# Two transformer blocks: memory projections done inside latent attention, and RWKV head sums as two rounded products of a split operand

## The reference, cut to what matters

```python
# first_block, each of the two layers: four kinds of attention, 4 heads of 64 channels each
out_mla = _causal_softmax_attention(q_full, k_full, v_mla, mla_scale)      # latent attention
mkv = einsum('bmd,dc->bmc', mem_n, w_mem_kv[l])                            # 256 memory rows -> keys, values
mem_logits = einsum('bhsd,bhmd->bhsm', heads(mq), mk) * head_scale         # mq: 256 columns of h_res @ w_in
out_mem = einsum('bhsm,bhmd->bhsd', softmax(mem_logits), mv)

# second_block, rwkv7_mixer: sums over the 64 channels of a head
kk = kk / max(sqrt(sum(kk * kk, -1)), 1e-12)                               # "norm"
y = wkv7_scan(r, decay, k, v, -kk, kk * a)
mu = mean(y, -1); var = mean((y - mu) ** 2, -1)                            # "mean", "var"
y = (y - mu) * rsqrt(var + GN_EPS) * gn_w + gn_b
y = (y + sum(r * k * r_k, -1) * v) * g                                     # "bonus"
```

## Time and profile before

| | |
|---|---|
| median of 3 runs | 3862.49 us (3860.55 to 3867.43) |
| the profiled execution | 3867.74 us, its span 3866.0 us |
| mean granted TensorE clock | 0.987 of 2.4 GHz |
| busy share of the span | PE 94%, DVE 41%, ACT 30%, POOL 26% |
| the pairs stage | about 2003 to 2760 us of the span |
| first-block layers, mla to mem | 454 to 578 us, and the same again from 1219 us |

### The profile page before, as it was taken

How to read it: one execution, slowest core, us unless ns; L and a number is a source line. 1 busy time by engine, 2 the same in 40 slices (tenths; PEclk the granted TensorE clock), 3 DMA queues, 4 the chain that set the end, 5 groups by cost and what they waited for, 6 DMA issues and landing times. The chain is left out here.

```text
span 3866.0 us, 69669 instructions
## 1 busy us (share of the span) xinstructions
PE 3647.5 (94%) x29888; PEld 2831.3 (73%) x29888; DVE 1590.0 (41%) x3026; ACT 1169.6 (30%) x2230; POOL 1008.1 (26%) x1676
## 2 busy tenths in 40 slices
PE   6899999998999999999889999999999999999998
PEld 5664667986656679779767777776787688888886
DVE  6634545445355444521764444444003452212123
ACT  2436333014363331201644444443111221101011
POOL 4120005231200051332022222221332133434342
PEclk9999999999999999999999999999899999999999
DMA  4131201211211012212110000000222211111122
GB/s 157 45 99 40 67 18 60 89 67 65 77 53 54 23 55 99 111 44 77 50 38 19 26 25 26 29 27 19 80 66 89 94 44 55 44 47 52 44 67 97
DMA packets 190204, 225.93 MB, mean 58 GB/s; under 512 B 20990, under 2 KB 168000, under 8 KB 187080
## 3 DMA queue, kind: packets, MB, share of 16 engines
q1 hardware_dynamic: 189896, 221.47, 17.5%
HBM read 188.89 MB, written 32.56 MB: 57 GB/s over the span
## 5 line engine op out<-in xcount | busy, mean ns | idle before, releaser
L200 POOL CAST weights_high<-weights_value 128x256 fp32r<-128x256 f32 x272 | 112.7, 463 | 1121.0 <-DMA weights_value<-in_w_in_dram 930.3
L218 PE MATMUL banks<-h_high,weights_high 128*128 128x512 f32 x608 | 238.5, 392 | 8.0 <-PEq L852 5.9
L218 PE MATMUL banks<-h_high,weights_low 128*128 128x512 f32 x608 | 236.7, 389 | 0.0
L4101 POOL CAST ffn_weights_high<-ffn_weights_value 128x256 fp32r<-128x256 f32 x256 | 103.8, 454 | 466.6 <-DMA ffn_weights_value<-in_w_ff_dram 356.3
L204 POOL TENSOR_TENSOR weights_low<-weights_value,weights_high 128x256 fp32r<-128x256 f32 x272 | 212.6, 818 | 2.8
L218 PE MATMUL banks<-ffn_in_high,ffn_weights_high 128*128 128x512 f32 x512 | 199.8, 390 | 5.1 <-PEq L4348 3.1
L4474 ACT ACTIVATE hidden_value<-banks 128x512 f32<-128x512 f32 x64 | 38.3, 598 | 537.9 <-PE banks L218 537.8
L218 PE MATMUL banks<-ffn_in_high,ffn_weights_low 128*128 128x512 f32 x512 | 199.2, 389 | 0.0
L218 PE MATMUL banks<-ffn_in_low,ffn_weights_high 128*128 128x512 f32 x512 | 199.2, 389 | 0.0
L218 PE MATMUL banks<-ffn_weights_high,hidden_high 128*128 128x512 f32 x512 | 199.2, 389 | 0.0
L218 PE MATMUL banks<-ffn_weights_low,hidden_high 128*128 128x512 f32 x512 | 199.2, 389 | 0.0
(11 more groups left out here) (498 smaller groups left out, 9274.3 us busy)
## 6 DMA issues: line engine op xcount, KB each, us to landing
ffn_weights_value<-in_w_ff_dram SPq DMA_DIRECT2D x32, 1024.0 KB, 5.4
weights_value<-in_w_in_dram SPq DMA_DIRECT2D x24, 1024.0 KB, 5.3
attention_scratch<-in_ada_w_dram SPq DMA_DIRECT2D x12, 1024.0 KB, 5.3
pair_weights_value<-in_w_in_dram SPq DMA_DIRECT2D x24, 512.0 KB, 4.1
ndow_weights_value<-in_w_in_dram SPq DMA_DIRECT2D x10, 1024.0 KB, 5.1
weights_value<-in_w_out_dram SPq DMA_DIRECT2D x8, 1024.0 KB, 5.3
gates_value<-in_w_in_dram SPq DMA_DIRECT2D x16, 512.0 KB, 5.2
first_mixed<-in_ada_w_dram SPq DMA_DIRECT2D x6, 1024.0 KB, 7.0
```

What stands on the lines that cost most here:

```text
L200: last = nc.gpsimd.tensor_copy(high[:, i, :], value[:, i, :])
L218: mm = nc.tensor.matmul(out, x, y, start=(first and i == 0 and j == 0), stop=(last and i == n - 1 and j == 2))
L4101: last = nc.gpsimd.tensor_copy(high[:, i], value[:, i])
```

## The change

**First block.** The stage `mem_project` is gone. Its six groups are a list `ahead`, given to the mla `pair_attention`: PE runs them right after `do_scores(0)`, in banks 4 to 7, and ACT moves all six after the exponents of unit 0. The 12 matmuls of `hold_clock` in that stage are gone. C_MQ is loaded and split one stage earlier, in `latent_heads`; C_MK and C_MV are loaded in the mla stage, C_GATE after the six groups. The memory queries and keys lie in other buffers.

**Pairs.** A head sum is four f32r matmuls 128x512: the rounded ones times the high and the low part of the operand. Each sum needs one ACT copy (rounding) and one DVE subtraction, 128x1024 each, ahead of it. PE's mean stands after `fill(3)` instead of before `fill(2)`, the variance after a `fill(2)` instead of before it. DVE's `logs` stand behind level 1, and ACT's square of y behind a later move.

```diff
+            if ahead:
+                sp.wait_ge(ahead_done, len(ahead))
+                w.load(sp, then_load)
...
+            def do_ahead(i):
+                chunk, pairs, n, move = ahead[i]
+                if i >= 4:
+                    pe.wait_ge(ahead_moved, i - 3)
+                    pe.wait_ge(w.loaded[chunk], 16)
+                gemm(nc, k.bank(4 + i % 4, n), pairs).then_inc(ahead_done, 1)
...
                     hold_clock(k, k.psum[:, 4, 0:P], quiet[0])
+                    for i in range(len(ahead)):
+                        do_ahead(i)
+                if it == 1 and ahead:
+                    pe.wait_ge(ahead_moved, len(ahead))
...
+                    for i, (chunk, pairs, n, move_ahead) in enumerate(ahead):
+                        act.wait_ge(ahead_done, i + 1)
+                        move_ahead(k.bank(4 + i % 4, n)).then_inc(ahead_moved, 1)
...
-SLOT_OF = {C_FL: 4, C_FQ: 0, C_FK: 1, C_FV: 3, C_OUT + 2: 2, C_OUT + 3: 3}
+SLOT_OF = {C_FL: 4, C_FQ: 0, C_FK: 1, C_FV: 3, C_MQ: 0, C_MK: 1, C_MV: 5, C_OUT + 2: 2, C_OUT + 3: 3}
...
-    mem_turned_bufs = [turned_bufs[0], flat(qt[:, 2:4, :])]
+    mem_turned_bufs = [turned_bufs[0], flat(qt[:, 0:2, :])]
...
+    def mem_query(tile, half):
+        rows = mem_queries[tile][:, half * HALF:(half + 1) * HALF]
+        return C_MQ, over_tokens(b, C_MQ, tile * P, P, half), HALF, moving(nc, "act", rows, -HEAD_SCALE)
+
+    def mem_key(tile):
+        pairs = [(W.value(C_MK)[:, i, tile * P:(tile + 1) * P], b.memt[:, i, :]) for i in range(KT)]
+        return C_MK, pairs, MEM, moving(nc, "act", b.mem_keys[:, tile, :])
+
+    ahead = [mem_query(tile, half) for tile in range(2) for half in range(2)] + [mem_key(tile) for tile in range(2)]
     pair_attention(k, "mla" + tag, (weight_bufs, turned_bufs), half_of(qt), half_keys(kt), own, pair_tile(2), CAUSAL_UNITS,
-                   diagonal=k.causal_add, prefetch=(C_MQ, C_MK), splits=(C_MQ,), w=W, turned_part=turned_part, quiet=(12, 0))
-
-
-    groups = paired(qt, C_MQ, 0, -HEAD_SCALE)
-    for tile in range(2):
-        groups.append((C_MK, (0, P, MEM), [(W.value(C_MK)[:, i, tile * P:(tile + 1) * P], b.memt[:, i, :]) for i in range(KT)],
-                       "dve", moving(nc, "dve", kt[:, tile, 0:MEM])))
+                   diagonal=k.causal_add, prefetch=(C_MK, C_MV), w=W, turned_part=turned_part, ahead=ahead, then_load=C_GATE)
+
+    def mem_half(p, e, t):
+        return mem_queries[p][64 * e:64 * e + 64, t * P:(t + 1) * P]
+
     mem_values = [([(b.memt[:, i, t * P:(t + 1) * P], W.value(C_MV)[:, i, :]) for i in range(KT)], values[:, t, :]) for t in range(2)]
-    project_stage(k, "mem_project" + tag, groups, W, loads=(C_MV,), prefetch=(C_GATE,))
-    pair_attention(k, "mem" + tag, (weight_bufs, mem_turned_bufs), half_of(qt), half_keys(kt), own, pair_tile(3), MEM_UNITS,
+    pair_attention(k, "mem" + tag, (weight_bufs, mem_turned_bufs), mem_half, half_keys(b.mem_keys), own, pair_tile(3), MEM_UNITS,
...
+            b.W.load(sp, C_MQ)
...
+            b.W.split(pool, (C_MQ,), weights_rounded, weights_split)
+            pool.wait_ge(weights_split, 1)
...
+    front_high, front_low = k.over("front_sums_high", [P, S], turned_at), k.over("front_sums_low", [P, S], level_at)
+    out_high, out_low = k.over("out_sums_high", [P, S], k.x_at + 4 * S), k.over("out_sums_low", [P, S], k.x_at + 8 * S)
...
-            def by_head_ones(key, p, src):
+            def by_head_ones(key, p, high, low):
                 b = back_bank(key, p)
                 for half in range(2):
-                    mm = nc.tensor.matmul(k.bank(b + half), k.head_ones, src[:, half * HALF:(half + 1) * HALF], start=True, stop=True)
+                    s = slice(half * HALF, (half + 1) * HALF)
+                    nc.tensor.matmul(k.bank(b + half), ones[:], high[:, s], start=True, stop=False)
+                    mm = nc.tensor.matmul(k.bank(b + half), ones[:], low[:, s], start=False, stop=True)
                 mm.then_inc(back_done, 1)
...
-                wait_freed(pe, "y", p)
-                by_head_ones("mean", p, ya)
+                pe.wait_ge(out_split, 2 * p + 1)
+                by_head_ones("mean", p, out_high, out_low)
             def variance(p):
-                pe.wait_ge(y_square, p + 1)
-                by_head_ones("var", p, yb)
+                pe.wait_ge(out_split, 2 * p + 2)
+                by_head_ones("var", p, out_high, out_low)
...
-                by_head_ones("norm", p, sq)
+                pe.wait_ge(front_split, 2 * p + 1)
+                by_head_ones("norm", p, front_high, front_low)
             def bonus_sum(p):
-                pe.wait_ge(bonus_in, p + 1)
-                by_head_ones("bonus", p, bonus[p % 3])
+                pe.wait_ge(front_split, 2 * p + 2)
+                by_head_ones("bonus", p, front_high, front_low)
...
+                fill(3)
                 if p:
                     mean(p - 1)
-                fill(2)
...
+                    fill(2)
                     if lev == 2 and p:
                         variance(p - 1)
-                    fill(2)
...
+            def norm_split(p):
+                dve.wait_ge(front_rounded, 2 * p + 2)
+                nc.vector.tensor_tensor(front_low[:], sq, front_high[:], ALU.subtract).then_inc(front_split, 1)
+
+            def bonus_split(p):
+                dve.wait_ge(front_rounded, 2 * p + 3)
+                nc.vector.tensor_tensor(front_low[:], bonus[p % 3], front_high[:], ALU.subtract).then_inc(front_split, 1)
+
+            def mean_split(p):
+                dve.wait_ge(out_rounded, 2 * p + 1)
+                if p + 1 < PAIRS:
+                    wait_freed(dve, "v_tok", p + 1)
+                nc.vector.tensor_tensor(out_low[:], ya, out_high[:], ALU.subtract).then_inc(out_split, 1)
+
+            def var_split(p):
+                dve.wait_ge(out_rounded, 2 * p + 2)
+                nc.vector.tensor_tensor(out_low[:], yb, out_high[:], ALU.subtract).then_inc(out_split, 1)
...
+                    mean_split(o)
                     centre(o)
+                if is_back:
+                    level(p, 1)
                 if is_front:
                     logs(f)
+                if is_out:
+                    var_split(o)
                 if is_back:
-                    level(p, 1)
                     level(p, 2)
...
+                    norm_split(f)
...
                     directions(f)
+                    bonus_split(f)
...
+                nc.scalar.mul(kk, kx, col(5, p))
+                nc.scalar.copy(front_high[:], sq).then_inc(front_rounded, 1)
...
+            def bonus_rounded(p):
+                act.wait_ge(bonus_in, p + 1)
+                nc.scalar.copy(front_high[:], bonus[p % 3]).then_inc(front_rounded, 1)
+
+            def mean_rounded(p):
+                wait_freed(act, "y", p)
+                nc.scalar.copy(out_high[:], ya).then_inc(out_rounded, 1)
+
+            def squared(p):
+                wait_freed(act, "mean", p)
+                step(nc.scalar.activation(yb, ya, ACT.Square))
+
+            def var_rounded(p):
+                nc.scalar.copy(out_high[:], yb).then_inc(out_rounded, 1)
...
+                        mean_rounded(o)
                     if p == 0:
                         act.wait_ge(oat_away, 16)
                     move("k_tok", p, k_tok)
                     move("v_tok", p, v_tok)
-                if is_out:
-                    wait_freed(act, "mean", o)
-                    nc.scalar.activation(yb, ya, ACT.Square).then_inc(y_square, 1)
-                if is_back:
...
+                                squared(o)
...
+                            var_rounded(o)
...
+                            bonus_rounded(f)
```

More of the change, by code:

```diff
@@ L807, in pair_attention @@
 def pair_attention(k, name, bufs, q, key, value, out, pair_units, diagonal=None, bias=None, bias_here=(),
-                   prefetch=(), w=None, splits=(), turned_part=None, late=(), late_weights=None, quiet=(0, 0)):
+                   prefetch=(), w=None, splits=(), turned_part=None, late=(), late_weights=None, quiet=(0, 0),
+                   ahead=(), then_load=None):
     nc = k.nc
@@ L1146, in first_block @@
         over_slot(3, scratch_at + 2 * S * 4, scratch_at + 4 * S * 4)
+        forget_at = k.next_place()
         w_high.append(k.sb("weights_forget_high", [P, KT, FORGET_COLS], F32R, ctx=own))
         w_two.append(k.twofold("weights_forget", [P, KT, FORGET_COLS], own))
+        over_slot(5, low_t_at, low_t_at)
+        mem_keys = k.over("mem_keys", [P, 2, MEM], forget_at, F32)
         gate_sigmoids = k.over("gate_sigmoids", [P, KT, S], heads_at, F32)
@@ L1978, in _ @@
             sp.sem_clear(arrived)
+            b.W.load(sp, C_MQ)
+        @block.gpsimd
+        def _(pool):
+            b.W.split(pool, (C_MQ,), weights_rounded, weights_split)
+            pool.wait_ge(weights_split, 1)
         @block.tensor
@@ L3017, in rwkv @@
     inv = k.sb("inverse", [P, S], ctx=scope)
+    turned_at = k.next_place()
```

(16 more changed lines are left out.)

23 lines of the change are left out of this document (13 added, 10 removed).

## The result

The changed kernel took 3837.16 us (median of 4 runs, 3829.41 to 3842.26) against 3861.52 before (3857.77 to 3867.43): the ratio is 0.9937, interval 0.9917 to 0.9957, so 24.4 us less with an interval of 17 to 32. The prediction was 3834 in a range of 3820 to 3850, and faster. Its profiled execution took 3837.41 us (span 3835.6); set against the profiled execution of before, 3867.74, that is 30.3.

What follows compares the result with a forecast made beforehand. PE, busy 94% of the span, was taken as the bound. 10.5 + 18.6 + 1.8 - 1.0 = 29.9, rounded to 28.5 for small waits, gave 3834 us from 3862.5, range 3820 to 3850.

Steps and rivals of the forecast that it cites:

- First block, 10.5: Two layers' mla and mem stages: clock matmuls, a 1.47 us wait and one stage edge go, 5.27 us each, 10.5 together.
- A sum gives 0.90: Head sums in the pairs: four f32r matmuls take PE 0.91 us instead of 1.81, so 0.90 less each.
- Inner pairs, 18.6: Pairs 1 to 6: four sums of 0.90 less a 0.5 us wait ahead of the mean, 3.1 each, 18.6 us gained.
- Pair 0, 1.8: Pair 0, with no output beside it: only the next pair's norm and bonus get shorter, 1.8 us gained.
- The ends, 1.0 lost: First pair's start loses 0.5; last pair's mean loses 1.4, 0.9 returned at the variance; behind the pairs even; 1.0 us lost.
- "even" behind the pairs: After the pairs: the last mean 1 us shorter, the variance waiting for about 2.3 us more chain work, no net change.
- the fall as a rival: Last pair: the wait ahead of the mean makes the clock fall earlier, costing up to 23 us, 3857; chance 0.05.
- another clock in the windows of the last pair: Last pair: a granted clock differing from before's profile was named as showing the forecast wrong; no size given.
- The other clock rival: Last pair and after: shorter sums keep the clock from falling, giving back up to 13 us, 3821; chance 0.08.
- More waits of half a microsecond: Pairs: each of the four sums costs PE the mean's 0.5 us wait, 12 us with the ends, 3846; chance 0.18.
- Operands late throughout: Seven pairs: every sum's copy and subtraction wholly exposed, each losing 1.36 us, 38 in all, 3890; chance 0.04.
- Sums no shorter: Pairs: f32r sums still take 1.81 us, so only the first block gains, 3852; chance 0.02.

Runs made afterwards that it cites:

- with the wait filled: Changed kernel with four gate steps put ahead of the mean in the last pair, sums left rounded; 3832.27 us, ratio 0.9932 to the kernel before.
- the plain ends: Changed kernel with six sums in the first pair and last two outputs again float32 products, without copy and subtraction; 3829.17 us, ratio 0.9926 to before.
- the rounded product alone: Changed kernel without the low product and DVE's subtraction of every sum, the copy kept; 3817.31 us, ratio 0.9889 to before.
- the first block's part alone: Kernel before with only the memory projections moved into the latent attention, pairs as before; 3842.74 us, ratio 0.9958, and again 3844.69, ratio 0.9961.
- with the keys in that wait: Changed kernel with the two groups of memory keys behind the transposes of unit 0; 3833.11 us, ratio 0.9934 to before.

## Why the prediction was right, and where its terms were off

**First block, 10.5.** Right in kind and size: 5.6 and 5.3 us at a clock of 1.00, C_MQ's split covered, the wait of 1.47 gone. It left out that the clock falls in these stages in some executions, 3 to 5 us each time.

**A sum gives 0.90.** Mis-sized: 0.79. I took the pitch of f32r matmuls among their like. In norm, bonus and variance the last of the four is followed only after 0.32 or 0.33 us and not 0.23, by a matmul on 64 rows; in the mean it is the first of the four, behind the wait, that is followed after 0.34.

**Inner pairs, 18.6.** 17.1 in the first two profiles, 15 of them by the pairs' part and 2 by idle time that changed with the first block; the shortfall is mostly that term. The wait ahead of the mean was forecast as 0.5 and is 0.36; none came at the variance, norm or bonus in an inner pair, as the plain sum of the rows had it. Pair 0, 1.8: 1.0 to 1.5 in the profiles.

**The ends, 1.0 lost.** This is the step that failed: they cost 5 to 10 us, and each of its three terms was too small.

The first pair's start was put at 0.5 lost and is 1.1 to 2.6 longer at a like clock. In the last pair the wait ahead of the mean came as forecast: 3.04 us of idle time instead of 0.86, so the mean starts 2.2 us later, as 2671.4 against 2669.23 had it. But the 0.9 were not given back at the variance: it starts 21.4 and 22.4 us behind the pair's first state products in the two profiles of the changed kernel, and 18.0 and 18.2 in the two undisturbed ones of before's code. And "even" behind the pairs was wrong: the last mean waits 1.25 us and the last variance 2.68, where before had 0 and 0.3.

What I did not count is the clock behind the first of these waits. Together 4 to 7 us are lost in the last pair against the 87 us of before's code without its long fall, and the waits are the larger part. The changed kernel's first profile has one fall only, at the mean, and loses 4.9 against the 86.61; of these the fall is 1.1 by an estimate, from 11.19 us between mean and variance here and 10.10 with the wait filled. Its second profile has three falls and loses 7.3. I had the fall as a rival, with a chance of 0.05 and 23 us; it came in each of the five profiles with that wait, but the clock is back within five us and falls again only here and there, so it costs 1 to 3 us by the same estimate. With it came a sign that I had named for being wrong, another clock in the windows of the last pair: 0.98 and 0.95, where before's first profile had 0.86. The other clock rival (the long fall given back by the shorter sums) is not shown: before's code was without that fall in three of its four profiles.

**The rivals.** More waits of half a microsecond in the inner pairs: out, of the four sums PE waits ahead of the mean alone. Of the four subtractions only the bonus's ran beside POOL's work, 1.74 to 1.76 us in place of 1.22, and PE did not wait for it. Operands late throughout: out. Sums no shorter: out.

With the measured terms the sum is 10.9 + 17.1 + 1.2, less 6 for the last pair and 1.1 to 2.6 for the first, 20.6 to 22.1, where the run gave 24.4 (17 to 32) and the forecast was 28.5. So the mechanism held in the middle of the pipeline and failed at its ends, and the forecast was within its range because that was 30 us wide and the ends are small beside the rest.

## What to carry to other kernels

In a stage whose engine is full, work added to idle engines can be nearly free (here about 2 us of 563) as long as each piece has other work between it and its consumer; the same edit in the first and last turn of a pipeline, where that work is missing, made PE wait. Treat the ends as kernels of their own: with the longer but unsplit product there the last pair was 4 to 7 us shorter, while the inner turns kept the gain. And before a stretch is called faster, look at its granted clock in more than one execution: the last pair seemed 6 us faster in the first comparison, and is about 6 us slower where before's code keeps its clock.

## What the runs showed of the hardware that was not expected

A wait of 3 us ahead of the mean in the last pair was followed at once by a lower granted clock in all five profiles that had it (0.66 to 0.68 over the five us from the mean on). A wait of 0.86 or 0.87 us at the same place was not, in six profiles (1.00 over the same five us): four of before's code, the plain ends and the rounded product alone. In two of these six, one of the first block's part alone and that of the rounded product, the clock fell eight or nine us further on all the same, so this wait is not the only place where it falls. In the mla stages the clock fell behind a wait of 1.50 us in some executions of the same code and not in others; with the keys in that wait it fell in none of four layers.

In the six inner pairs of the changed kernel's first profile an f32r matmul is followed after 0.32 or 0.33 us by a float32 matmul on 64 rows of the array (64*64 or 64*128; 143 times), 0.1 more than the pitch, and after 0.23 by a float32 one on all 128 rows (128*128; 42 times). So the tenth does not come with the change of type alone.

In the same profile the bonus's subtraction on DVE took 1.74 to 1.76 us in the seven pairs in which it met work of POOL, and 1.22 in the eighth. The two subtractions of POOL that it met took 1.59 and 1.72 us in an inner pair, where those that met no work of DVE took 0.73.
